# Moving projection blocks within one group of the token mixer, and exchanging the order of the tail

## The reference, cut to what matters

```
h = rmsnorm(x, g_mix);  proj = h @ w_in               # 1024 -> 10272 columns
lru_in, lru_gate, z, xbc, dt, gate_a, gate_b = split(proj)
u = causal_conv4(lru_in); hs = rg_lru(u)              # a linear recurrence over tokens
y_a = hs * gelu(lru_gate)
xs, B, C = split(silu(causal_conv4(xbc)))
y_b = ssd_chunked(xs * dt, A, B, C, state) + D * xs   # 8 groups of 4 heads, chunks of 128
y_b = grouped_rmsnorm(y_b * silu(z))
x = x + (sigmoid(gate_a) * (y_a @ w_a) + sigmoid(gate_b) * (y_b @ w_b)) @ w_out
```

## Time and profile before

| | us |
|---|---|
| median of 3 runs (1095.74 to 1096.97) | 1096.93 |
| the profiled execution's own time | 1097.6 |
| its span, first to last instruction | 1095.8 |
| prologue, to the first group | 48.6 |
| mixer, eight groups | 549.4 |
| branch products and routing | 160.0 |
| experts | 265.0 |
| tail | 72.8 |

### The profile page before, as it was taken

The page is one execution under the profiler, slowest core; times in us unless marked ns, Lnnn a source line. Parts: engine busy times, 40 slices in busy tenths (PEclk is TensorE's granted clock), DMA queues, the critical chain, the costliest instruction groups (busy, mean ns, idle before and its releaser), DMA issues.

```text
span 1095.8 us, 16848 instructions
## 1 busy us (share of the span) xinstructions
PE 953.8 (87%) x5389; PEld 699.4 (64%) x5389; DVE 599.1 (55%) x1069; ACT 411.7 (38%) x687; POOL 172.1 (16%) x214
## 2 busy tenths in 40 slices
PE   5597888978889788897886999998999999999874
PEld 3486776867778576686765999775444444443553
DVE  3675875758757587575875654263333342432424
ACT  3454562635636456264564432153111111111312
POOL 0043241232412324123240000010000000000000
PEclk9798998979889899898996999988999999999988
DMA  7171351813617136171361850591999999999001
GB/s 185 40 180 45 103 156 38 215 43 95 164 38 212 46 93 166 38 212 46 95 179 45 230 167 25 177 370 39 351 394 384 384 389 392 378 390 333 0 1 43
DMA packets 208599, 188.51 MB, mean 172 GB/s; under 512 B 8000, under 2 KB 166392, under 8 KB 208568
## 3 DMA queue, kind: packets, MB, share of 16 engines
q1 hardware_dynamic: 207352, 187.12, 53.3%
q10 hardware_dynamic: 1216, 0.98, 0.3%
HBM read 176.88 MB, written 11.21 MB: 172 GB/s over the span
## 4 chain that ended last, share of the span: by engine, by line
PE 64%; DVE 16%; ACT 9%; issue 7%; DMA 1%; DVEq 1%; ACTq 0%; SPq 0%
PE bank L1685 11%; PE bank L1389 6%; PE bank L1713 5%; PE bank L1390 5%; PE bank L1641 5%; PE bank L1391 5%; PE bank L1549 4%; PE bank L1648 3%; PE bank L1464 3%; PE bank L1578 3%; PE bank L1733 3%; DVE wlo L961 2%; PE bank L1553 2%; DVE ii L1092 2%; ACT whi L699 2%
## 5 line engine op out<-in xcount | busy, mean ns | idle before, releaser
L1389 PE MATMUL bank<-h_hi,whi 128*128 128x288 f32 x640 | 212.0, 331 | 28.2 <-DVE wlo L961 28.1
L1390 PE MATMUL bank<-h_lo,whi 128*128 128x288 f32 x640 | 202.9, 317 | 0.0
L1391 PE MATMUL bank<-h_hi,wlo 128*128 128x288 f32 x640 | 201.8, 315 | 0.0
L1389 PEld LDWEIGHTS bank<-h_hi,whi 128*128 128x128 f32 x640 | 134.4, 210 | 47.3 <-DVE wlo L961 33.6
L1390 PEld LDWEIGHTS bank<-h_lo,whi 128*128 128x128 f32 x640 | 134.3, 210 | 0.5
L1391 PEld LDWEIGHTS bank<-h_hi,wlo 128*128 128x128 f32 x640 | 133.9, 209 | 0.0
L1284 DVE TENSOR_TENSOR xT<-xT,bank 128x288 f32<-128x288 f32 x128 | 49.5, 450 | 152.4 <-PE bank L1648 152.4
L699 ACT ACTIVATE whi<-wb 128x1024 fp32r<-128x1024 f32 x82 | 86.8, 1060 | 95.6 <-PE bank L1391 92.1
L961 DVE TENSOR_TENSOR wlo<-wb,whi 128x1024 fp32r<-128x1024 f32 x82 | 103.4, 1262 | 20.2 <-ACT whi L699 12.4
L887 ACT ACTIVATE Gs<-bank 128x512 f32<-128x512 f32 x16 | 9.6, 597 | 145.1 <-PE bank L1685 145.1
L1641 PE MATMUL bank<-pick,htok 96*128 96x256 f32 x240 | 59.0, 387 | 1.1 <-ACT yb L866 1.1
(11 more groups left out here) (349 smaller groups left out, 1632.8 us busy)
## 6 DMA issues: line engine op xcount, KB each, us to landing
wb<-in_w SPq DMA_DIRECT2D x80, 1024.0 KB, 8.6
wb<-in_w_in SPq DMA_DIRECT2D x80, 512.0 KB, 4.0
wb3a<-in_w SPq DMA_DIRECT2D x16, 1024.0 KB, 8.6
arena<-in_state_ssd SPq DMA_DIRECT2D x16, 512.0 KB, 5.6
out_new_ssd_s<-arena SPq DMA_DIRECT2D x16, 512.0 KB, 5.8
wb<-in_w_br_ssd SPq DMA_DIRECT2D x16, 512.0 KB, 3.9
wb<-in_w_br_lru SPq DMA_DIRECT2D x8, 512.0 KB, 3.8
wb<-in_w_out SPq DMA_DIRECT2D x8, 512.0 KB, 5.0
```

Of the source, the lines that this page charges most:

```text
L1389: mm(bP[i % 2][:, 0:T], hi, h_hi[:, k, :], start=(k == 0), stop=False)
L1390: mm(bP[i % 2][:, 0:T], hi, h_lo[:, k, :], start=False, stop=False)
L1391: ins = mm(bP[i % 2][:, 0:T], lo, h_hi[:, k, :], start=False, stop=(k == KC - 1))
```

## The change

On TensorE, block 8 goes ahead of the third transposes; block 9 goes from behind the second half of the states to between `y_diag` and the first state transposes; block 0 of the next group goes ahead of the last state transposes and block 1 ahead of the norm's sum. ACT and DVE follow: ACT takes blocks 0 and 1 of the next group out of PSUM within the group (`evac(g, 10)` and `evac(g, 11)`, with the large halves of the next blocks 2 and 3), and the loop no longer begins with them. DVE makes the small half 9 ahead of the third tokens, 10 behind the third weights, `yb` and `fin` and half 11 ahead of the LRU chain, half 12, `conv` 0 of the next group and half 13 at the end of the group ahead of the norm. The last group is written out apart, without the next group's work. POOL's `Dg` waits for the last use of the old `Dg` (CU_ready) in place of the end of `y_state`. In the tail DVE does `gate_out(j - 1)` and `gate_sum(j - 1)` before `gate_in(j)`, and ACT squares j-1 before the sigmoid of j.

```diff
--- before.py
+++ after.py
...
-        CU_ready, CU_free = sig("CU_ready", 6), sig("CU_free", 6, 1)
+        CU_ready, CU_free = sig("CU_ready", 6, 3), sig("CU_free", 6, 1)
...
-                        + ["sig0"] + [n for j in range(1, 8) for n in (f"sig{j}", f"sy{j - 1}")] + ["sy7", "yrt", "out0", "out2", "out4"])
+                        + ["sig0"] + [n for j in range(1, 8) for n in (f"sy{j - 1}", f"sig{j}")] + ["sy7", "yrt", "out0", "out2", "out4"])
         dve_end = Steps(sem("dve_end"), [n for p in range(4) for n in (f"x3_{p}", f"x3_{p + 4}", f"hg{p}", f"hg{p + 4}")] + ["t0"]
-                        + [n for j in range(1, 8) for n in (f"t{j}", f"x4_{j - 1}", f"xg{j - 1}", f"acc{j - 2}") if n != "acc-1"]
-                        + ["x4_7", "xg7", "acc6", "acc7", "yrs", "out1", "out3", "out5"])
+                        + [n for j in range(1, 8) for n in (f"x4_{j - 1}", f"xg{j - 1}", f"acc{j - 1}", f"t{j}")]
+                        + ["x4_7", "xg7", "acc7", "yrs", "out1", "out3", "out5"])
         xg = ya
         gt = [gl[:], Gs[:, 0:T]]
...
-                pool.wait_ge(YO_ready.sem, YO_ready.at(g, 0))
+                pool.wait_ge(CU_ready.sem, CU_ready.at(g, -3))
...
+            def evac(g, i):
+
+                act.wait_ge(projected.sem, projected.at(g, i + 1))
+                large(g, i + 2)
+                n = i % 10
+                act.wait_ge(conv_done.sem, conv_done.at(g, i + 1 - 5 if i < 10 else n + 1))
+                act.wait_ge(stashed.sem, stashed.at(g, i + 1 - 5 if i < 10 else n + 1))
+                ch(act_f(pads[n][:, 3:SMP], bP[n % 2][:, 0:NP], ACT.Copy))
+                ch.tell(act_f(new_tokens(pads[n], 3), samples(bP[n % 2][:, NP:T]), ACT.Copy), proj_free, i + 1)
+
+            def group(g, last):
 
...
-                evac(0)
-                evac(1)
                 act.wait_ge(YO_ready.sem, YO_ready.at(g, 0))
                 act.wait_ge(y_done.sem, y_done.at(g, 0))
                 silu(0)
-                evac(2)
+                evac(g, 2)
                 silu(1)
-                evac(3)
+                evac(g, 3)
                 silu(2)
-                evac(4)
+                evac(g, 4)
                 silu(3)
...
                 raw(7, gl[:])
+                raw(8, ga[:, ds(g, 1), :].rearrange("p o t -> p (o t)"))
                 decay_rows(2)
                 decay(2)
                 act.wait_ge(m2_ready.sem, m2_ready.at(g, 1))
                 ch.tell(act_f(TT[:], TT[:], ACT.Sqrt), m_ready, 1)
-                raw(8, ga[:, ds(g, 1), :].rearrange("p o t -> p (o t)"))
                 from_T(4, sprev[:], 256)
                 from_T(5, sT[:, 0:4, :].rearrange("p b n -> p (b n)"), 512)
                 from_T(6, sT[:, 4:8, :].rearrange("p b n -> p (b n)"), 512)
+                raw(9, gb[:, ds(g, 1), :].rearrange("p o t -> p (o t)"))
                 from_T(7, sT[:, 0:4, :].rearrange("p b n -> p (b n)"), 512)
+                if not last:
+                    evac(g, 10)
                 from_T(8, sT[:, 4:8, :].rearrange("p b n -> p (b n)"), 512)
-                raw(9, gb[:, ds(g, 1), :].rearrange("p o t -> p (o t)"))
                 act.wait_ge(y_done.sem, y_done.at(g, 1))
                 ch.tell(act_f(tw[:, :, 0:T], yb[:, ds(2 * g, 2), :], ACT.Square), sq_ready, 1)
+                if not last:
+                    evac(g, 11)
                 act.wait_ge(CB_ready.sem, CB_ready.at(g, 2))
                 ch.tell(act_f(zs[:, 0, :], bCB[:, 0:T], ACT.Sqrt, bias=EPS, scale=1.0 / 256), CB_free, 1)
                 ch.tell(act_f(gl[:], gl[:], ACT.Gelu_apprx_tanh), gelu_ready, 1)
+
+            evac(0, 0)
+            evac(0, 1)
+            with act.Fori(0, G - 1) as g:
+                ch.enter(g, 11)
+                group(g, False)
+            ch.peel(G - 1)
+            group(G - 1, True)
...
             for j in range(8):
-                act.wait_ge(dve_end.sem, dve_end.at(f"t{j}"))
-                if j >= 2:
-                    act.wait_ge(dve_end.sem, dve_end.at(f"x4_{j - 2}"))
-                ch.step(act_f(sg[j % 2], gt[j % 2], ACT.Sigmoid), act_end, f"sig{j}")
                 if j >= 1:
                     square_x4(j - 1)
+                act.wait_ge(dve_end.sem, dve_end.at(f"t{j}"))
+                ch.step(act_f(sg[j % 2], gt[j % 2], ACT.Sigmoid), act_end, f"sig{j}")
...
+            def conv(g, i, wcol, stride, bcol, at, n=0):
+
+                dve.wait_ge(proj_free.sem, proj_free.at(g, i + 1 + 10 * n))
+                dve.wait_ge(pad_hist.sem, pad_hist.at(g, i + 1 + 5 * n))
+                dve.wait_ge(silu_done.sem, silu_done.at(g, i - 1 + 4 * n))
+                x, y = pads[i], cv[i % 2]
...
+            small(0, 2)
+            conv(0, 0, C_SW, 32, C_SB, 0)
+            small(0, 3)
+
+            def group(g, last):
 
...
-                small(g, 2)
-                conv(0, C_SW, 32, C_SB, 2 * g)
-                small(g, 3)
-                conv(1, C_SW, 32, C_SB, 2 * g + 1)
+                conv(g, 1, C_SW, 32, C_SB, 2 * g + 1)
                 small(g, 4)
-                conv(2, C_SW, 32, C_SB, g + 16)
+                conv(g, 2, C_SW, 32, C_SB, g + 16)
                 small(g, 5)
-                conv(3, C_SW, 32, C_SB, g + 24)
+                conv(g, 3, C_SW, 32, C_SB, g + 24)
                 small(g, 6)
-                conv(4, C_LW, 8, C_LB, g)
+                conv(g, 4, C_LW, 8, C_LB, g)
                 small(g, 7)
...
                 weights(0)
                 weights(1)
+                small(g, 9)
                 tokens(2)
                 diff(2)
                 weights(2)
-                small(g, 9)
-
+                small(g, 10)
+
+                dve.wait_ge(Y_ready.sem, Y_ready.at(g, 2))
+                for j in range(2):
+                    ins = v.scalar_tensor_tensor(out=yb[:, ds(2 * g + j, 1), :].rearrange("p o t -> p (o t)"), in0=xbc[j][:],
+                                                 scalar=Dt[:, ds(2 * g + j, 1)],
+                                                 in1=bY[j][:, 0:T], op0=ALU.mult, op1=ALU.add)
+                    ch(ins) if j == 0 else ch.tell(ins, Y_free, 2)
+
+                dve.wait_ge(CU_ready.sem, CU_ready.at(g, 4))
+                dve.wait_ge(state_out, g * 48 + 1)
+                for j in range(2):
+                    ch(v.tensor_scalar(fin[:, j, :], bCU[:, 256 * j:256 * j + P],
+                                       ex[:, j, P - 1:P], None, ALU.mult))
+                    ins = v.tensor_tensor(fin[:, j, :], fin[:, j, :], bCU[:, 256 * j + P:256 * j + 2 * P], ALU.add)
+                    ch(ins) if j == 0 else ch.tell(ins, CU_free, 4)
+
+                small(g, 11)
                 dve.wait_ge(m_ready.sem, m_ready.at(g, 1))
...
-                dve.wait_ge(Y_ready.sem, Y_ready.at(g, 2))
-                for j in range(2):
...
-                small(g, 10)
...
-                small(g, 11)
+                if not last:
+                    small(g, 12)
                 new_states(1)
                 new_states(2)
                 new_states(3)
                 ch(v.tensor_copy(hfin[:, 0:1, ds(g, 1)].rearrange("p b o -> p (b o)"), rr[:, NP - 1:NP]))
                 ch(v.tensor_copy(hfin[:, 1:9, ds(g, 1)].rearrange("p b o -> p (b o)"), rr[:, NP + NT - 1:T:NT]))
 
+                if not last:
+                    conv(g, 0, C_SW, 32, C_SB, 2 * g + 2, n=1)
+                    small(g, 13)
                 dve.wait_ge(CB_free.sem, CB_free.at(g, 1))
...
             for j in range(8):
-                gate_in(j)
                 if j >= 1:
                     gate_out(j - 1)
-                if j >= 2:
-                    gate_sum(j - 2)
+                    gate_sum(j - 1)
+                gate_in(j)
             gate_out(7)
-            gate_sum(6)
             gate_sum(7)
...
+            pe.sem_inc(CU_ready.sem, 3)
...
                 token_major(1)
                 cum_rows(1)
                 proj(g, 7)
+                proj(g, 8)
                 token_major(2)
                 cum_rows(2)
-                proj(g, 8)
 
                 pe.wait_ge(xdte_ready.sem, xdte_ready.at(g, 1))
                 pe.wait_ge(T_free.sem, T_free.at(g, 3))
                 mm(bT[:, 0:256], btok[:, 0, :], xdte[:, 0, :], start=True, stop=True).then_inc(T_ready.sem, 1)
                 pe.wait_ge(Y_free.sem, Y_free.at(g, 1))
                 y_diag(0)
+                y_diag(1)
+                proj(g, 9)
                 state_T(0, 0)
-                y_diag(1)
                 pe.wait_ge(YO_free.sem, YO_free.at(g, 0))
                 for j in range(2):
                     mm(bYO[:, 160 * j:160 * j + P], sprev[:, j * P:(j + 1) * P], xbc[3][:, P:2 * P], start=True, stop=True)
+                y_diag(2).then_inc(Y_ready.sem, 1)
                 state_T(0, 1)
-                y_diag(2).then_inc(Y_ready.sem, 1)
 
                 pe.wait_ge(xdte_ready.sem, xdte_ready.at(g, 3))
                 pe.wait_ge(CU_free.sem, CU_free.at(g, 3))
@@ -1512,22 +1531,21 @@
```

(47 more changed lines are left out.)

32 lines of the change are left out of this document (removed).

## The result

| | before | after |
|---|---|---|
| median of 4 runs, us | 1096.95 | 1066.11 (1063.87 to 1067.93) |
| ratio, 95% interval | | 0.972 (0.970 to 0.974) |
| the profiled execution's own time / span, us | 1097.6 / 1095.8 | 1067.93 / 1066.1 |
| mixer and branch stage, us | 709.4 | 694.4 |
| tail, us | 72.8 | 58.1 |

The change made the kernel 30.8 us faster where 56.5 were forecast, and the time lies just outside the range (1020 to 1066). The two profiled execution times differ by 29.7 us: 14.7 of it is the tail and 15.0 the mixer with its branch stage. The mixer should have given 43.

What follows compares the result with a forecast made beforehand. No mixer engine is full; a chain of waits across engines sets the 68.6 us group, lengthened by TensorE's low clock and POOL's lock. Gains 37.1 + 6.0 + 13.4 = 56.5 off 1097.6 give 1041 us, range 1020 to 1066.

Steps and rivals of the forecast that it cites:

- The mixer should have given 43: Mixer: period 63.3, 5.3 less than 68.6, seven times gives 37.1 us; 6.0 more in the last group.
- the forecast ones: TensorE's new waits: 3.9 us before block 4, 2.4 before the token states, 0.9 before y_state 1.
- as walked: ACT, from the end of block 6 to large half 9: 9.16 us, unchanged by the edit.
- the rival said: POOL's lock moves along: Dg starts first, the LRU chain stays as long as before; 1050 us, chance 0.10.
- my 1.1 on the path: In the POOL lock case, the LRU chain needs 11.0 of 9.9 us, adding 1.1 per group, 9 in all.
- 13.4 were forecast: Tail gain 13.4 us (12 to 15); step bound by TensorE at 0.4 + 4.05, one first wait of 3.5 staying.
- The clock* is the unknown: TensorE's clock behind new waits: 2.8 us a group added to the full-clock period, ends 0 and 7.3.
- The walk at full clock: One new group laid out step by step, all blocks at 2.4 GHz: next conv 0 at 60.4, period about 60.5 us.
- The three places that I priced: Clock prices per group on TensorE: block 4 0.9 us, block 9 1.2, block 0 of the next group 0.7.
- last group: From conv 1 of the last group to br_hi, 61.2 us before: pieces shorten alike, no block 0; gain 6.0.
- the clock takes the gain: Rival: blocks 4, 9 and 0 all get the dear price; period 65.5 to 68, 1057 to 1079 us, chance 0.16.
- the dear price: The costlier clock level for a TensorE block: about 2.6 us more, wholly at 1.2 GHz, against 1.45 more.

Runs made afterwards that it cites:

- e10: The changed kernel with unread products filling TensorE's three waits (e2) and new-state products over 128 rows (e9): 1028.77 us, ratio 0.936 to the kernel before.
- e9: The changed kernel with new-state products over 128 rows in place of 32, the added rows zero: 1045.88 us, ratio 0.952 to the kernel before.
- e2: The changed kernel with extra products, overwritten or never read, in TensorE's three waits: 1049.33 us, ratio 0.956 to the kernel before.
- e3: The changed kernel with the norm's sum ahead of next block 1, the norm ahead of conv 0 and half 13, the root ahead of evac(g, 11): 1039.25 us.
- e4: The changed kernel with DVE's loop of seven groups written out, constant addresses and no branch back: 1043.66 us, ratio 0.950 to the kernel before.
- e7: The changed kernel with the edits of e3 and e4 together: 1036.41 us, ratio 0.944 to the kernel before.
- e12: The changed kernel with the edits of e7 and e9, and 14 overwritten products ahead of the token states: 1004.40 us, ratio 0.915 to the kernel before.
- e11: The changed kernel with the edits of e3 and e9 together: 1031.19 us, ratio 0.939 to the kernel before.
- e5: The kernel of e2 with seven more never-read products of 192 columns between the small products of each y_state: 1062.86 us, ratio 0.967 to the kernel before.

## Why the prediction was wrong, by its own steps

**Right: the mechanism and the direction.** In the group from 248.82 the waits of TensorE are within about 0.2 us of the forecast ones, the waits for `fin` and for the third rows are gone, and ACT's stretch from block 6 to the large half 9 takes 9.2 (276.3 to 285.47) as walked. L1137, the former L1128 of the earlier trace rows, is 0.49 in every group:

```profile
L1137 DVE TENSOR_TENSOR yb<-yb,arena x8: 491/492/492, 108.6 to 571.3; 128x320 f32 x7, 128x320 f32<-128x320 f32 x1
```

**Right, with a twist: POOL.** `Dg` moved into the LRU chain, as the rival said; L1116 is 2.22 where it could be 0.46, beside this row of POOL's timeline:

```profile
300.86 3.09 POOL L624 TENSOR_TENSOR arena<-cumT,cst 32x1152 f32<-32x1152 f32 x1 [0.33 <-POOL pad L621]
```

But L1117 takes 0.46 and DVE is idle for 2.00 behind the chain, so it costs nothing. The rule of the Trainium skill, "SBUF — State Buffer", section "Who interferes with whom", agrees with these rows on the lock; my 1.1 on the path for that case does not, since the chain was short enough otherwise.

**Right: the tail.** 14.7 where 13.4 were forecast; its step is 4.22 us (1034.39 to 1038.61), bound by TensorE, where 0.4 + 4.05 were taken. TensorE waits there for `ya` twice (3.5, and 2.27 at the end) where one wait was forecast.

**Wrong: "*The clock* is the unknown", taken at 2.8 a group.** The walk at full clock gave 60.4 for the group that took 67.5 (248.82 to 316.31). Along the same steps the 7.1 are (the last column is the price that the prediction gave to the clock):

| place | us over the walk | forecast |
|---|---|---|
| half 13, waiting for block 1 of the next group, which runs low | 1.4 | 0 |
| branch of DVE's loop ahead of `conv` 1 | 1.0 | 0 |
| blocks 4 and 5 behind the wait of 3.69 | 1.0 | 0.9 |
| token states to the end of block 0 | 2.1 | 1.9 |
| `y_state` 1 | 0.6 | 0 |
| behind it: DVE waits 0.7 for the new states, and 0.3 ahead of `conv` 0 | 1.0 | 0 |

The three places that I priced came out at 3.1 together, where 2.8 was taken. That their sum is right is partly luck: the second part fell on block 9 and on the token states and `y_diag` ahead of it, and block 0, priced at 0.7, cost nothing. The mis-sized term is what I left out of it: I gave the clock a price only where a block follows a wait. The longest low stretch starts at the end of `y_state` 1 and runs through the new states and block 1, with TensorE busy. It costs 2.4: 1.4 at half 13, 0.3 of the 0.6 at `y_state` 1 and 0.7 of the last 1.0. The rest of these two rows is not the clock's: at full clock, too, `y_state` 1 takes 2.0 until DVE goes on (240.41 to 242.40) where the walk had 1.7, and DVE stands 0.35 ahead of `conv` 0, which the walk had left out. So the clock cost 5.5 in this group and not 2.8, the branch, which the walk forgot, 1.0, and these two 0.6. e10 agrees: with the low time brought from 18.2 to 4.0, its step is 5.4 shorter than that of the kernel after. Over the seven steps the miss is 7 x (5.3 - 1.6) = 26, nearly the whole difference between 56.5 and 30.8. The other three terms (last group 4.8 for 6.0, tail, branch stage 1.3 longer) cancel within about 1 us. The case that came is the rival "the clock takes the gain" (1057 to 1079), though not by the dear price for the three blocks that it named.

**What shows the cause.** That the clock is on the path is shown by e9 (rows alone, 20.2 us less) and e2 (more work, 16.8 us less), and the two kinds of step in the kernel after agree. That it is most of the missing part is shown by e10, where four of six steps are 61.4 with no low clock left on the path. That the order of the norm and DVE's chain are on the path as well is shown by e3 and e4, each alone; put together in e7 they give hardly more than e3, and in e12, with the clock up, the step is 58.1. How e12's further gain parts between them is not shown. Not shown either is why the products of 32 rows go with the lower clock: in e9 the new states mostly still run low (their median is 1061 ns, the least 592), and the low time falls around them and behind the token states. A rival is that the rows only shift the moment at which the clock changes, so that every step comes out like the shorter ones of the kernel after. Against it, the rows lower the low time on three different kernels (18.2 to 13.7 in e9, 9.1 to 4.0 in e10, 10.3 to 7.4 in e11), but no run rules it out.

## What to carry to other kernels

When independent work is moved into TensorE's waits, price the clock for everything that follows on TensorE, not only for the block behind each wait: here 7 to 10 us at 1.2 GHz stood behind products of four columns, with TensorE busy throughout. If the granted clock is low where TensorE is busy, it is worth trying to give small products more rows (zeros) or to fill a wait with products that nobody reads; both made this kernel faster with more work (e9, e2). Products put between small ones, where TensorE was not waiting, made it slower (e5). In a walk of one step of a loop, count the loop's own branch back on each engine, and put what the next step waits for (here the norm) ahead of the work that was drawn forward.

## What was not expected of the hardware

Zero rows made the kernel faster: the same products over 128 rows in place of 32 took 20.2 us off (0.952 against 0.972 of before). With the edits of e12 all products of the mixer's six steps ran at a granted clock of 1.00, against 0.88 for mixer and branch stage after, although waits of 2.32 us remained. And DVE's loop costs more than its branch: 0.97 us from the norm to the next `conv` in the loop against 0.04 written out (e4), and 3.79 against 3.35 for a `conv` with its half, whose operations follow each other more closely there.
